# Squares and sums of the attention output on ScalarE, epsilon on GpSimd, and VectorE's small steps of two heads interleaved

## The chip, the cores and the metric

The kernel runs on one core of one Trainium2 chip. The metric is the device time in microseconds of one execution, the median over the runs. TensorE, VectorE, ScalarE and GpSimd each work through their own list of instructions in order and wait for one another by semaphores; the profile calls them PE (with PEld for its weight loads), DVE, ACT and POOL.

## The reference, cut to what matters

The program is a backbone of two layers over 256 context tokens and 1024 latent tokens, width 1024. Each layer mixes its tokens by four parallel groups and then runs a SwiGLU network. The change touches one of the groups, differential attention with four heads, 32 wide in queries and keys and 64 wide in values:

```
s = einsum('bhcqd,bhckd->bhcqk', q, k) * 32 ** -0.5      # c = 0, 1: two score maps per head
p = softmax(s, axis=-1)
w = p[:, :, 0] - lam * p[:, :, 1]
o = einsum('bhqk,bhkd->bhqd', w, v)
# then, per token and head, over the 64 values:
y = o * rsqrt(mean(o * o) + 1e-5) * g_subln * (1 - lam_init)
```

Latent queries read all 1280 keys. Context queries read the 256 context keys, and only in layer 0. All else of the layer (projections, retention, pooling, convolution, the network) is untouched.

## The kernel before, in words

Attention runs in three stretches ("runs"): in layer 0 the context tokens (2 tiles of 128 queries, 256 keys) and then the latent tokens (8 tiles, 1280 keys), in layer 1 the latent tokens alone (8 tiles). Within a run each engine has a hardware loop over the tiles; the first tile, and on TensorE the last, is written out ahead of or behind it. One lap handles the four heads of one tile, and each engine has its own fixed order of work, with older heads mixed in. `back(r, h, n)` names the head n before head h of tile r.

For one head the work passes through the engines like this:

- TensorE computes both score maps into PSUM (`scores`, L998).
- VectorE takes the maximum of each map (`maxima`, L2128), and for the first map it makes the exponential's bias from it (L2135). For the second map ScalarE makes the bias itself (L1559).
- ScalarE takes the exponentials and, by its accumulator, their sums (`exps`, L1565).
- VectorE (`combine`, one head later) takes the reciprocals of both sums (L2142), the ratio `beta` (L2143), and one pass over the keys that makes the weights of both maps together (L2147), released by semaphore `w`. The factor 1/sum of the first map is left for later, in `rinv` (L2150, once a tile).
- TensorE transposes the weights, 128 keys at a time (`turn`, L1016), ScalarE copies them out of PSUM (L1576), TensorE multiplies them with the values (`values`, L1028), and ScalarE copies the head's output (L1583).

When the four heads of a tile are done, its output is finished within the next lap, between that lap's heads 2 and 3:

- TensorE brings it to token-major form (`token_major`, L1036), in head 2.
- VectorE multiplies by `rinv` (`out_sum`, L2154), squares (L2157), sums over 64 (L2158), scales and adds epsilon (L2159), all behind the second maximum of head 2.
- GpSimd raises to the power -1/2 (L2699).
- VectorE multiplies by it (`out_norm`, L2166), behind the first maximum of head 3.
- TensorE transposes the result (`turn_out`, L1055), ScalarE writes its high 16-bit part with the gain (`out_hi`, L1587), VectorE the low part (`out_lo`, L2171).

TensorE's order within head 3 is: transposes for head 1, second score map of head 3, `turn_out`, first transposes for head 2, first score map of the next tile, then the modulation's matmuls (L926, a projection for a later part of the layer, fed in small pieces; in layer 0 heads 0, 1 and 3 have a piece, in layer 1 all four) and the values of head 1. The modulation of head 3 waits for `out_lo`, because both use one PSUM bank. A second small piece of the modulation (L933) stands ahead of the scores, and ScalarE copies its rows (L1501).

Semaphores for waits within an engine go through a small class, `Chain`: `link` raises the engine's own semaphore at the end of an instruction and waits for it at once; `enter` and `leave` keep its count over a hardware loop, whose raises per lap are stated as `per`.

## Time and profile before

| | us |
|---|---|
| Median of 3 runs | 3162.82 |
| Lowest and highest | 3156.35, 3166.67 |
| The profiled execution | 3156.76 |
| Its span in the profile | 3154.9 |
| TensorE busy | 2883.1 |
| VectorE busy | 1951.7 |
| ScalarE busy | 1238.2 |
| GpSimd busy | 561.6 |
| Mean granted TensorE clock, share of full speed | 0.961 |

The span is that of the instructions in the trace; the time of the execution lies 1.9 us above it. In the trace every time is counted from the span's start. Attention lies at 480 to 731 us (layer 0) and 2136 to 2352 us (layer 1). A line of the timeline gives the start, the duration, the engine, the line of the kernel, the operation, what it writes and reads, how many instructions were merged, and in brackets how long the engine had been idle before it and what ended that.

### The profile page before, as it was taken

To read this page: it belongs to the slowest core of one execution; us is meant where nothing else is said; L and a number is where in the kernel's file an instruction comes from. 1 tells how busy PE (TensorE), PEld (TensorE's weight loads), DVE (VectorE), ACT (ScalarE), POOL (GpSimd) and SP (SyncE) were. 2 spreads that over 40 slices of the span, in tenths; PEclk is the share of its full clock that TensorE was granted. 3 is DMA by queue.
4 is the path that set the end of the run, shared out by engine and by line. 5 is a ranking of instruction groups with operands and counts; after the bars stand their busy time and mean duration, and the time that the engine had idled before them with its cause. 6 is when DMAs were issued, how large, how long until landed. Compare 5 with 4: busy or idle time off the path is not lost.

```text
span 3154.9 us, 47187 instructions
## 1 busy us (share of the span) xinstructions
PE 2883.1 (91%) x17730; PEld 1617.4 (51%) x17730; DVE 1951.7 (62%) x2706; ACT 1238.2 (39%) x2368; POOL 561.6 (18%) x449
## 2 busy tenths in 40 slices
PE   5999887888899999999998899987889999999997
PEld 3555643554545556757755554544554434444443
DVE  5976786882575304626646686778864673374765
ACT  5212456773543213313324311447753542231332
POOL 0021010001318101202212004010003160121211
PEclk8999996999999999999999799999989999999998
DMA  5211111221143321111141311113322432111133
GB/s 211 74 41 36 36 46 70 86 78 67 55 147 133 107 87 41 41 41 50 45 147 41 143 44 41 44 42 112 109 79 80 137 103 76 51 56 52 54 140 115
DMA packets 69316, 248.95 MB, mean 79 GB/s; under 512 B 9248, under 2 KB 10016, under 8 KB 69152
## 3 DMA queue, kind: packets, MB, share of 16 engines
q1 hardware_dynamic: 68000, 241.44, 22.6%
q10 hardware_dynamic: 1152, 5.24, 0.4%
q8 instruction: 112, 1.84, 0.2%
q14 instruction: 52, 0.43, 0.0%
HBM read 221.75 MB, written 19.92 MB: 77 GB/s over the span
## 4 chain that ended last, share of the span: by engine, by line
PE 60%; issue 20%; DVE 11%; ACT 5%; DMA 2%; POOL 1%; SPq 0%; DVEq 0%; POOLq 0%; ACTq 0%
PE PS L801 38%; PE PS L970 16%; DVE wlo L1925 3%; PE PS L822 2%; DVE R L2102 1%; ACT whi L1418 1%; DVE R L2089 1%; PE PS L1175 1%; ACT SW L1776 1%; DMA R<-in_w_ada 1%; DMA stage<-in_w_gu 1%; ACT X L1535 1%; ACT R L1533 1%; DVE X L2378 1%; PE PS L1220 1%
## 5 line engine op out<-in xcount | busy, mean ns | idle before, releaser
L801 PE MATMUL PS<-R,whi 128*128 128x512 f16 (+1 forms) x4992 | 1359.2, 360 | 47.1 <-DVE wlo L1925 30.8
L801 PE MATMUL PS<-R,wlo 128*128 128x512 f16 (+1 forms) x2496 | 896.4, 359 | 0.0
L801 PEld LDWEIGHTS PS<-R,whi 128*128 128x128 f16 x4992 | 487.5, 99 | 550.8 <-issue 51.7
L970 PE MATMUL PS<-R,whi 128*128 128x256 f16 (+2 forms) x2352 | 510.2, 326 | 0.3 <-DVE wlo L1938 0.3
L1925 DVE SCALAR_TENSOR_TENSOR wlo<-stage,whi 128x1024 f16<-128x1024 f32 (+1 forms) x204 | 283.4, 1390 | 362.0 <-ACT whi L1418 361.1
L801 PEld LDWEIGHTS PS<-R,wlo 128*128 128x128 f16 x2496 | 246.2, 99 | 242.5 <-issue 10.7
L970 PE MATMUL PS<-R,wlo 128*128 128x256 f16 (+2 forms) x1176 | 319.1, 326 | 0.0
L970 PEld LDWEIGHTS PS<-R,whi 128*128 128x128 f16 x2352 | 230.1, 98 | 152.5 <-DVE wlo L1938 0.8
L1418 ACT ACTIVATE whi<-stage 128x1024 f16<-128x1024 f32 (+1 forms) x204 | 210.4, 1032 | 135.3 <-PE PS L801 85.0
L2128 DVE TENSOR_REDUCE tiny<-PS 128x1 f32<-128x1280 f32 (+1 forms) x144 | 197.1, 1369 | 37.4 <-PE PS L998 35.7
L1954 DVE TENSOR_TENSOR X<-X,PS 128x256 f32<-128x256 f32 (+2 forms) x294 | 150.8, 549 | 93.4 <-PE PS L970 93.2
L2616 POOL TENSOR_TENSOR X<-X 128x512 f32<-128x512 f32 (+1 forms) x89 | 121.6, 1370 | 384.4 <-ACT X L1818 290.9
L1565 ACT ACTIVATE R<-PS,tiny 128x1280 f32<-128x1280 f32 (+1 forms) x144 | 177.8, 1235 | 9.9 <-DVE tiny L2135 7.6
L2743 POOL TENSOR_TENSOR X<-stage 128x512 f32<-128x512 f32 x28 | 36.0, 1287 | 799.0 <-DMA stage<-in_w_gu 799.0
L2284 DVE SCALAR_TENSOR_TENSOR R<-X,small,R 128x1024 f32<-128x1024 f32 (+1 forms) x180 | 173.4, 1012 | 1.8
L970 PEld LDWEIGHTS PS<-R,wlo 128*128 128x128 f16 x1176 | 115.1, 98 | 76.0
L1436 ACT ACTIVATE whi<-X 128x512 f16<-128x512 f32 x112 | 70.0, 627 | 193.1 <-PE PS L970 90.9
L998 PE MATMUL PS<-R 128*128 128x512 f16 (+1 forms) x400 | 111.3, 362 | 34.6 <-ACT R L1576 22.9
L1016 PE MATMUL PS<-ident,R 128*128 128x128 f32 x656 | 106.1, 293 | 35.3 <-DVE R L2147 33.6
L1938 DVE SCALAR_TENSOR_TENSOR wlo<-X,whi 128x512 f16<-128x512 f32 x112 | 91.4, 818 | 51.6 <-ACT whi L1436 51.6
L1576 ACT ACTIVATE R<-PS 128x512 f32<-128x512 f32 (+1 forms) x200 | 97.2, 519 | 52.1 <-PE PS L1016 44.7
L2147 DVE SCALAR_TENSOR_TENSOR R<-R,tiny 128x1280 f32<-128x1280 f32 (+1 forms) x72 | 103.2, 1433 | 8.3
(227 smaller groups left out, 3570.3 us busy)
## 6 DMA issues: line engine op xcount, KB each, us to landing
stage<-in_w_gu SPq DMA_DIRECT2D x120, 512.0 KB, 3.8
X<-in_w_ada SPq DMA_DIRECT2D x60, 512.0 KB, 3.3
stage<-in_w_down SPq DMA_DIRECT2D x48, 512.0 KB, 3.4
stage<-in_w_in SPq DMA_DIRECT2D x44, 512.0 KB, 3.3
stage<-in_w_out SPq DMA_DIRECT2D x32, 512.0 KB, 3.2
h_save<-R SPq DMA_DIRECT2D x24, 640.0 KB, 5.3
R<-h_save SPq DMA_DIRECT2D x24, 640.0 KB, 4.9
T<-in_w_ada SPq DMA_DIRECT2D x20, 512.0 KB, 3.6
```

What stands on the lines that cost most here:

```text
L801: last = mm(slot(into, t0, t1)[:, c0 - t0:c1 - t0], w[:, j, k, :], row, start=(k == 0 and q == 0), stop=(k == K - 1 and q == 2))
L970: last = mm(s_bank(nf, t, o, n), w[:, j, k0 + k, :], row, start=(k == 0 and x == 0), stop=(k == PAIRS - 1 and x == 2))
L998: last = mm(slot(c)[:, k0:k1], Qst[:, 2 * h + c, bass.ds((t_first + r) * P, P)], Kst[:, 2 * h + c, k0:k1], start=True, stop=True)
L1016: last = nc.tensor.transpose(o[:, i * P:(i + 1) * P], Wt[h % 2][:, (k0 + i) * P:(k0 + i + 1) * P], ident[:, :])
L1418: A(whi[:, j, 0:K, :], stage[:, j, 0:K, :], ACT.Copy, scale=WS).then_inc(S["w_hi"], 1)
L1565: A((P1, P2)[c][h % 2][:, 0:keys], slot(c)[:, 0:keys], ACT.Exp, scale=SCORE, bias=nbias[:, h % 2, c:c + 1], accum_out=den[:, h % 2, c:c + ...
L1925: STT(wlo[:, j, 0:K, :], stage[:, j, 0:K, :], WS, whi[:, j, 0:K, :], ALU.mult, ALU.subtract).then_inc(S["w_lo"], 1)
L1954: last = TT(s_temp(l, dst)[:, o:o + w], s_temp(l, src)[:, o:o + w], s_bank(nf, t, o, w), ALU.add)
L2128: red = RED(smax[:, h % 2, c:c + 1], slot(c)[:, 0:keys], AX.X, ALU.max)
L2147: STT(Wt[h % 2][:, 0:keys], P2[h % 2][:, 0:keys], beta[:, 0:1], P1[h % 2][:, 0:keys], ALU.mult, ALU.add).then_inc(s("w"), 1)
L2284: STT(acc, src, wv, acc, ALU.mult, ALU.add).then_inc(S["conv"], 1)
L2616: TT(xrow(0)[:, a0:a1], xrow(0)[:, a0:a1], xrow(2 + d % 2)[:, a0:a1], ALU.add).then_inc(S[used], 1)
```

## The change

ScalarE gets the squares and sums of the tile's output (`out_squares`): four instructions, one for each head, Square with a scale of 1/8, so that the accumulated sum is already the mean over 64. They stand at the start of head 3 in ScalarE's order, ahead of the copies of older heads. GpSimd adds epsilon before its power. VectorE's `out_sum` keeps only its multiplication.

VectorE's order changes too. The reciprocal of the head before now stands between the first maximum and its bias, the ratio behind the bias, and `rinv` between the ratio and the pass that makes the weights. The waits within the engine are split into a raise (`mark`) and a later wait (`reach`), so that another instruction can stand between. `out_norm` moves from ahead of the weights' pass to behind it.

```diff
+    def mark(self, ins):
+        ins.then_inc(self.s, 1)
+        self.k += 1
+        return self.k
+
+    def reach(self, k):
+        self.eng.wait_ge(self.s, self.base + k)
...
 ScalarE
+                def out_squares(r):
+                    act.wait_ge(S["o_sum"], r + (done + 1))
+                    for h in range(HA):
+                        last = A(AO[:, 1, h, :], AO[:, 0, h, :], ACT.Square, scale=0.125, accum_out=st8[:, 0, h:h + 1])
+                    last.then_inc(S["o_sq"], 1)
+
                 def tile(r, first=False):
                     for h in range(HA):
+                        if h == 3 and not first:
+                            out_squares(r - 1)
                         if h == 3 or not first:
                             headed(*back(r, h, 3))
...
                 pv_copy(nt - 1, 3)
+                out_squares(nt - 1)
                 out_hi(nt - 1)
...
 VectorE
-                    own.link(red)
+                    return own.mark(red)
+
+                def bias(r, h, maximum):
+                    n = 4 * r + h
+                    own.reach(maximum)
                     if not (isinstance(r, int) and n < 2):
                         dve.wait_ge(s("exps"), 2 * n - 3 + before("exps"))
                     TS(nbias[:, h % 2, 0:1], smax[:, h % 2, 0:1], -SCORE, lamv[:, 12 + l:13 + l],
                        ALU.mult, ALU.add).then_inc(s("nbias"), 1)
 
-                def combine(r, h):
+                def inverse(r, h):
+
+                    dve.wait_ge(s("exps"), 2 * (4 * r + h) + 2 + before("exps"))
+                    return own.mark(nc.vector.reciprocal(rec[:, h, :], den[:, h % 2, :]))
+
+                def combine(r, h, inverted):
 
                     n = 4 * r + h
-                    dve.wait_ge(s("exps"), 2 * n + 2 + before("exps"))
-                    own.link(nc.vector.reciprocal(rec[:, h, :], den[:, h % 2, :]))
-                    own.link(STT(beta[:, 0:1], den[:, h % 2, 0:1], lamv[:, 10 + l:11 + l], rec[:, h, 1:2], ALU.mult, ALU.mult))
+                    own.reach(inverted)
+                    ratio = own.mark(STT(beta[:, 0:1], den[:, h % 2, 0:1], lamv[:, 10 + l:11 + l], rec[:, h, 1:2], ALU.mult, ALU.mult))
+                    if h == HA - 1:
+                        own.mark(TS(rinv, rec[:, :, 0], 1.0 / XS, None, ALU.mult))
+                    own.reach(ratio)
...
                     STT(Wt[h % 2][:, 0:keys], P2[h % 2][:, 0:keys], beta[:, 0:1], P1[h % 2][:, 0:keys],
                         ALU.mult, ALU.add).then_inc(s("w"), 1)
-                    if h == HA - 1:
-                        own.link(TS(rinv, rec[:, :, 0], 1.0 / XS, None, ALU.mult))
...
-                    dve.wait_ge(S["o_sum"], r + (done + 1))
-                    own.link(TT(AO[:, 1, :, :], AO[:, 0, :, :], AO[:, 0, :, :], ALU.mult))
-                    own.link(RED(st8[:, 0, 0:4], AO[:, 1, :, :], AX.X, ALU.add))
-                    TS(st8[:, 1, 0:4], st8[:, 0, 0:4], 1.0 / DV, 1e-5, ALU.mult, ALU.add).then_inc(S["o_var"], 1)
...
                     for h in range(HA):
-                        maxima(r, h, 0)
+                        maximum = maxima(r, h, 0)
+                        if h or not first:
+                            inverted = inverse(*back(r, h, 1))
+                        bias(r, h, maximum)
+                        if h or not first:
+                            combine(*back(r, h, 1), inverted)
                         if h == 3 and not first:
                             out_norm(r - 1)
-                        if h or not first:
-                            combine(*back(r, h, 1))
                         maxima(r, h, 1)
...
 GpSimd
                     with pool.Fori(0, nt) as r:
-                        pool.wait_ge(S["o_var"], r + (done + 1))
+                        own.enter(r, 1)
+                        pool.wait_ge(S["o_sq"], r + (done + 1))
+                        own.link(TT(st8[:, 1, 0:4], st8[:, 0, 0:4], epsv[:, 1:2].to_broadcast([P, 4]), ALU.add))
                         TT(st8[:, 2, 0:4], st8[:, 1, 0:4], nhalf[:, 0:1].to_broadcast([P, 4]),
                            ALU.pow).then_inc(S["o_pow"], 1)
+                    own.leave(nt, 1)
```

## Rows read from the trace of the kernel before

**Rows 1.** The page, busy time by engine over the whole span.
```profile
PE 2883.1 (91%) x17730; PEld 1617.4 (51%) x17730; DVE 1951.7 (62%) x2706; ACT 1238.2 (39%) x2368; POOL 561.6 (18%) x449
```
**Rows 2.** Windows between two GpSimd powers: stretch, length, busy by engine, clock, DMA.
```profile
632.55:657.22 24.67, 19.73 (x212) 13.29 (x210) 21.96 (x32) 19.26 (x41) 1.00 (x1) 1.00 0.25 90
657.22:683.45 26.23, 21.22 (x212) 14.56 (x210) 21.97 (x32) 19.27 (x41) 1.01 (x1) 0.93 0.24 85
2203.08:2227.84 24.76, 20.31 (x231) 13.82 (x228) 22.00 (x32) 19.42 (x42) 1.01 (x1) 1.00 0.33 112
```
**Rows 3.** Timeline of one lap of layer 1, around head 3.
```profile
2201.44 0.70 PE L998 MATMUL PS<-R 128*128 128x512 f16 x3
2201.47 0.41 DVE L2154 TENSOR_TENSOR R<-PS,st 128x256 f32<-128x256 f32 x1
...
2203.08 1.49 DVE L2128 TENSOR_REDUCE tiny<-PS 128x1 f32<-128x1280 f32 x1
2203.08 1.01 POOL L2699 TENSOR_TENSOR st<-st,tiny 128x4 f32<-128x4 f32 x1 [25.20 <-DVE st L2159]
2203.34 0.20 ACT L1565 ACTIVATION_READ_ACCUMULATOR R<-PS,tiny 128x1 f32 x1
...
2204.08 0.28 ACT L1501 ACTIVATE SW<-PS 128x128 f32<-128x128 f32 x1 [0.55 <-PE PS L1028]
...
2205.16 0.16 DVE L2142 RECIPROCAL st<-tiny 128x2 f32<-128x2 f32 x1
...
2205.42 1.33 ACT L1565 ACTIVATE R<-PS,tiny 128x1280 f32<-128x1280 f32 x1
...
2205.71 0.39 PE L1055 MATMUL PS<-ident,R 128*128 128x128 f32 x2
2205.71 1.55 DVE L2147 SCALAR_TENSOR_TENSOR R<-R,tiny 128x1280 f32<-128x1280 f32 x1
...
2207.40 0.65 PE L1016 MATMUL PS<-ident,R 128*128 128x128 f32 x4 [1.30 <-DVE R L2147]
...
2208.03 0.70 PE L998 MATMUL PS<-R 128*128 128x512 f16 x3
...
2208.58 0.47 DVE L2171 SCALAR_TENSOR_TENSOR R<-PS,small,R 128x256 f32 x1
...
2209.16 0.65 PE L926 MATMUL PS<-X,cpad 128*32 128x128 f32 x16 [0.43 <-issue]
```
**Rows 4.** The same timeline, from head 0 to head 1 of the following tile.
```profile
2213.72 0.21 ACT L1565 ACTIVATION_READ_ACCUMULATOR R<-PS,tiny 128x1 f32 x1
...
2214.42 0.70 PE L998 MATMUL PS<-R 128*128 128x512 f16 x3
...
2215.16 1.49 DVE L2128 TENSOR_REDUCE tiny<-PS 128x1 f32<-128x1280 f32 x1 [0.62 <-PE PS L998]
...
2218.41 1.33 ACT L1565 ACTIVATE R<-PS,tiny 128x1280 f32<-128x1280 f32 x1
```
**Rows 5.** Timeline of ScalarE in the retention stage of layer 0.
```profile
411.11 0.24 ACT L1776 ACTIVATE SW<-T 128x64 f32<-128x64 f32 x1
...
411.35 0.24 ACT L1776 ACTIVATE SW<-T 128x64 f32<-128x64 f32 x1
```
**Rows 6.** View of the exponential's line: duration min/median/max, first and last start.
```profile
L1565 ACT ACT_TABLE_LOAD  x2: 1283/1283/1283, 479.2 to 2136.2; - x2
```
**Rows 7.** Groups of GpSimd instructions by shape: count, busy us, mean ns, idle before.
```profile
L2616 POOL TENSOR_TENSOR X<-X 128x512 f32<-128x512 f32 x69 | 86.2, 1251 | 304.4 <-ACT X L1818 242.7 <-ACT X L1522 60.0
...
L2720 POOL TENSOR_TENSOR R<-R 128x256 f32<-128x256 f32 x4 | 2.7, 672 | 0.3
```
**Rows 8.** Timeline at the end of layer 1's attention run.
```profile
2349.86 0.42 DVE L2166 TENSOR_TENSOR R<-R,st 128x256 f32<-128x256 f32 x1 [1.12 <-POOL st L2699]
```
**Rows 9.** Timeline of the context run's one lap, layer 0.
```profile
499.93 0.19 ACT L1565 ACTIVATION_READ_ACCUMULATOR R<-PS,tiny 128x1 f32 x1
...
501.30 0.43 DVE L2166 TENSOR_TENSOR R<-R,st 128x256 f32<-128x256 f32 x1 [0.56 <-POOL st L2699]
```

More of the change, by code:

```diff
@@ L269, in build @@
               "slot_free act_own dve_own pool_own h_in out_done y_sq_ready y_sq_used h_sq_ready h_sq_used sumsq mean_sq root diag spread inv u_scaled u_hi u_done h_rows h_saved h_back "
-              "o_ps o_sum o_var o_pow o_norm ot_ps ot_hi ot_done").split()}
+              "o_ps o_sum o_sq o_pow o_norm ot_ps ot_hi ot_done").split()}
         S |= {n: sem(n) for n in PER_LAYER}
@@ L2155, in out_sum, with out_norm @@
                        rinv[:, :].rearrange("p (h e) -> p h e", e=1).to_broadcast([P, HA, DV]), ALU.mult).then_inc(S["o_sum"], 1)
+                def out_norm(r):
                     dve.wait_ge(S["o_sum"], r + (done + 1))
-                    own.link(TT(AO[:, 1, :, :], AO[:, 0, :, :], AO[:, 0, :, :], ALU.mult))
-                    own.link(RED(st8[:, 0, 0:4], AO[:, 1, :, :], AX.X, ALU.add))
-                    TS(st8[:, 1, 0:4], st8[:, 0, 0:4], 1.0 / DV, 1e-5, ALU.mult, ALU.add).then_inc(S["o_var"], 1)
-                def out_norm(r):
                     dve.wait_ge(S["o_pow"], r + (done + 1))
@@ L2186, in tile @@
                             out_lo(r - 1)
-                per = 4 + 8 + 1 + 2
+                per = 4 + 8 + 1
                 tile(0, first=True)
@@ L2194, in attend @@
                 own.leave(nt - 1, per)
-                combine(nt - 1, HA - 1)
+                combine(nt - 1, HA - 1, inverse(nt - 1, HA - 1))
                 out_sum(nt - 1)
```

## The prediction

> **What bounds the kernel now.** Read the page first: TensorE is busy for 91% of the span, VectorE for 62% and ScalarE for 39% [rows 1]. The change touches only the attention stage, so the question is what bounds that stage; the view of windows cut from one GpSimd root to the next gives it. A lap (one tile of 128 queries, four heads) of 1280 keys takes 24.67 us in layer 0 and 24.76 us in layer 1, VectorE busy for 22.0 of it, ScalarE for 19.3 and TensorE for 20 [rows 2]. Nobody is full: the lap is a ring of waits, to be read from the timeline of one lap.
>
> In the plain heads the ring runs through TensorE and ScalarE. The exponential's accumulator is read until 2213.92, the next scores start at 2214.42, and then come values, transposes and their copies until the next exponential of the same kind at 2218.41 [rows 4]. The span from one end to that start is 4.49 us; with 1.41 us of exponential and read it makes 5.90 us a head. VectorE waits 0.62 us for TensorE in it, so making VectorE faster there buys nothing.
>
> Head 3 is the other kind: 24.76 - 3 x 5.90 = 7.06 us, 1.16 us more. There VectorE holds the output sum (2201.47), the squares, sums and epsilon, and only then the maximum at 2203.08, though the scores ended at 2202.14. Its weights come at 2205.71 + 1.55 = 2207.26, and TensorE, idle for 1.30 us, starts the transposes at 2207.40. Then the scores of the next tile start at 2208.03, the low output part ends on VectorE at 2209.05, and the modulation's matmuls, which wait for it, start at 2209.16 [rows 3]. VectorE's chain sets this head twice.
>
> **What the change does, in layer 1's lap.** Three VectorE instructions leave each tile, which filled the 1.20 us from 2201.88 to the maximum at 2203.08. (a) The maximum of head 3 no longer waits for them. It starts when the scores are there: 2201.44 + 0.70 = 2202.14, plus the 0.04 us that the same pair shows in head 1 (2215.12 to 2215.16) [rows 3, 4], so 2202.18, and ends at 2203.67, where it ended at 2204.56.
>
> (b) From the maximum's end to the weights it was 1.15 us. The normalising multiply moves behind the weights (0.34 us net, by the 0.41 of an instruction of its shape less an overlap of 0.08), and the reciprocal (0.19 from its start to its follower's) slips into the wait for the maximum [rows 3]. That leaves 0.62 us: weights from 2204.29 to 2205.85. If the interleaving hides nothing it is 2206.05; I take the first. The reciprocal now stands ahead of the bias and waits for an exponential of the head before, read until 2203.54, 0.13 us before it is needed; the bias is needed at 2205.42 only, so this wait costs nothing up to some 1.5 us. The Trainium skill (VectorE: DVE Perf Modes, The DRAIN you can't avoid) says that instructions on VectorE gain nothing by being issued without semaphores between them; by that the weights would end at 2206.05 and the modulation start some 0.1 us later.
>
> (c) ScalarE gains four squares with sums. The trace has this operation on the same 128x64 shape: pairs of square and read start every 0.24 us (411.11, 411.35) [rows 5], so four take 0.97 us. They stand behind the exponential read until 2203.54, where ScalarE used to be idle for 0.55 us. The last sum is there at 2204.50, and the copies that started at 2204.08 start at 2204.40 [rows 3]: 0.32 us late. Everything behind them on ScalarE moves by that, so exponential (3,0) starts at 2205.74 and is read until 2207.15. Between 0 (all idle) and 0.97 (no idle) I take 0.32; layer 0's laps without a modulation at head 2 have less idle, so up to 0.7 there, but they also have the longer wait of TensorE to win back, and I price them alike.
>
> (d) GpSimd gains the addition of epsilon, 128x4, which no row shows. Additions there take 672 ns for 256 columns and 1251 for 512 [rows 7]: 2.26 ns a column, so about 0.1 us for 4. From above, the only 128x4 row is the power, 1.01 us [rows 3]. I take 0.1 plus 0.07 for the link, because two rows of the same operation point there, and keep 1.01. Then the power runs from about 2204.75 to 2205.76. The Trainium skill (GPSIMD Engine Reference, Performance versus the Vector engine) puts two software dispatch hops on each instruction here and makes elementwise work VectorE's; that speaks for the dearer end, and with it the root would come at 2206.7.
>
> (e) The normalising multiply starts when weights and root are there, 2205.8, and ends at 2206.22. TensorE turns the output 0.14 us later (the delay that 2207.26 to 2207.40 shows), for 0.39 us, and the transposes of head 2 follow until about 2207.25. Scores of the next tile: 0.50 us behind the exponential's read [rows 4], 2207.65, where it was 2208.03. The second maximum of head 3 runs 2206.22 to 2207.7, the low output part 2207.65 to 2208.1, and no longer holds the modulation, which follows the scores' 0.70 us with a small overlap, at about 2208.29. It was 2209.16 [rows 3]: **0.87 us a lap**. The check by the ring: head 3 is now 5.90 + 0.32 = 6.2 us, where it was 7.06. What is late next is the TensorE and ScalarE ring itself, which is why the saved 1.2 us of VectorE work and the 0.2 us in each other head are not worth more.
>
> Where each layer runs eight tiles, seven laps hold this work of the tile before: 14 x 0.87 = 12.2 us. What stands outside it:
> - Three run ends, where the chain lies bare (VectorE waits 1.12 us for the root [rows 8]). Before, 1.20 us passed from the output sum's end (2201.88) to the power's start (2203.08); now 0.05 to ScalarE, 1.06 of squares, 0.08 to GpSimd, 0.17 of addition: 1.36. That is +0.16 each, +0.5 in all; with the dear addition +3.2.
> - The one lap of the context run (256 keys). VectorE waited 0.56 us for the root even before, at 501.30. The exponential ahead of the squares is read until 500.12, so the root comes at 500.12 + 0.97 + 0.08 + 0.17 + 1.01 = 502.35 and the multiply 1.1 us later than before [rows 9]: +1.1.
>
> Net without the clock: -12.2 + 0.5 + 1.1 = -10.6 us.
>
> **The clock.** A lap at mean granted clock 1.00 takes 24.67 us, the next one at 0.93 takes 26.23 [rows 2]. Six of the 12 full laps between one tile's root and the next have 0.93, and cost 0.8 to 1.6 us each, 7.8 together; each time the fall to the lower level (1.2 GHz) follows head 3, where TensorE idled longest. That idle time, 1.30 + 0.43 us in layer 1, shrinks by about 0.9. So between none and all six go; I take three, -4.5 us, since the fall came only in some laps with the same idle time. Forecast: **-15 us**, 0.5%. Against the profiled execution (3156.76 us, span 3154.9) that is 3142; against the median of 3162.82, which is 6 us above the profiled one, 3148.
>
> **Rivals.**
> 1. The root comes late. If the addition costs 1.01 us the multiply starts at 2206.7, and because it stands in VectorE's order ahead of the second maximum and on TensorE ahead of the transposes, everything of (e) moves with it: maximum to 2208.6, low part to 2209.05, modulation at 2209.16, just as before. Gain per lap 0, run ends and context +5, clock unchanged: about 3168. For it: the 1.01 us row. Against: the two rows of additions. 13%.
> 2. ScalarE's squares are paid in full (0.97 instead of 0.32): the lap gains 0.2 us, 3 us in all; with run ends and the context lap 3161. For it: ScalarE lies in the ring of every head. Against: the 0.55 us of idle before 2204.08. 9%.
> 3. The lap gains, but the lower clock level comes in more laps than six: without any change of the clock the time is 3152, with two laps more 3155, with all 12 (+6 x 1.4) 3161. For it: other stretches of the head get denser waits. Against: the fall follows the longest idle, which shrinks. 12%.
> 4. The other side: the square needs another activation table than the exponential. One load is 1.28 us [rows 6], two a lap 2.57 us on ScalarE inside the ring. From 0.9 us of added ScalarE time per lap the sign turns; here 2.57 - 0.87 = 1.7 us more in 14 laps, and 6 us at the context lap and run ends: 3193. Against: the exponential's line has two loads in the whole execution, one for each layer, though squares run on ScalarE later under the same table. 4%. The Trainium skill (ScalarE: Activation LUTs, Table sets) names square in no set but says that cheap functions are in every one; the two loads agree with that.
>
> **Chances.** Forecast 62%, rivals 13, 9, 12 and 4%. 0.3% (9.5 us) is what a measurement of this kernel can tell from no change, so faster means below 3153.3. Faster: nearly all of the forecast, a third of rivals 2 and 3: 0.68. Same 0.26, slower 0.06. Range: the low end is the forecast with all six clock falls gone (-10.6 - 7.8 = -18.4, 3144) less 5 us for medians that differ by such; the high end, 3161, takes in rivals 2 and 3, and leaves out 1 and 4.
>
> **What would show it.** In the timeline of a lap of layer 1: maximum of head 3 within 0.8 us of the output sum's start; four squares every 0.24 us, ending about 1 us behind the read; an addition of about 0.1 us on GpSimd (at 1 us rival 1 holds); the copies at head 3 about 0.3 us later against the read than now; TensorE's idle before the transposes of head 2 gone; laps of about 23.9 us at clock 1.00, plain heads still 5.90. In the table by lap, fewer than six at 0.93. Loads still two on the exponential's line. It is wrong if plain heads change length, or if the multiply behind the weights is found waiting for GpSimd.

## The result: 0.4% slower

The changed kernel takes 3174.49 us (median of 6 runs, 3168.87 to 3176.29). The kernel before, run beside it, takes 3162.86 us (6 runs, 3155.49 to 3166.67). The ratio is 1.004, with an interval of 1.0026 to 1.0053: slower by 11.6 us. The prediction said 3148 with a range up to 3161, and gave slower a chance of 0.06. It was wrong, in sign too.

The profiled execution of the changed kernel took 3176.29 us (span 3174.5), 19.5 more than the profiled one of before. The page's busy times first:

```profile
PE 2896.6 (91%) x17730; PEld 1626.4 (51%) x17730; DVE 1928.7 (61%) x2652; ACT 1251.8 (39%) x2512; POOL 579.5 (18%) x467
```

VectorE is busy for 23 us less and ScalarE for 14 us more than in [rows 1], as planned. The work was moved. The time went elsewhere. Cut by stage, from the exponential's table load to the end of the last low output part, layer 0's attention grew from 251.5 to 261.5 us and layer 1's from 215.9 to 222.3; all the rest grew by 3.1. So the laps have to be read. The windows from one GpSimd power to the next, as in [rows 2]:

```profile
641.37:668.73 27.36, 22.12 (x208) 15.12 (x208) 21.01 (x28) 19.97 (x49) 2.32 (x3) 0.88 0.22 81
2219.87:2246.33 26.46, 21.73 (x226) 14.68 (x226) 21.01 (x28) 20.07 (x50) 2.32 (x3) 0.94 0.29 104
2273.20:2298.50 25.30, 20.24 (x226) 13.84 (x226) 20.98 (x28) 20.07 (x50) 2.32 (x2) 1.00 0.30 109
```

The one lap at clock 1.00 takes 25.30 us, where it was 24.76 and should have been 23.89. VectorE is busy for 1.0 us less in it and still the lap is longer. And 11 of the 12 laps now hold a fall of the clock, where it was 6; some stand at 0.88. The timeline of head 3 of a layer 1 lap shows why, against [rows 3].

```profile
2215.36 0.41 DVE L2180 TENSOR_TENSOR R<-PS,st 128x256 f32<-128x256 f32 x1
2216.09 1.49 DVE L2145 TENSOR_REDUCE tiny<-PS 128x1 f32<-128x1280 f32 x1 [0.32 <-PE PS L1006]
2217.35 0.25 ACT L1601 ACTIVATE R<-R 128x64 f32<-128x64 f32 x1
...
2218.18 1.55 DVE L2175 SCALAR_TENSOR_TENSOR R<-R,tiny 128x1280 f32<-128x1280 f32 x1
2218.30 0.26 ACT L1509 ACTIVATE SW<-PS 128x128 f32<-128x128 f32 x1
2218.48 1.31 POOL L2726 TENSOR_TENSOR st<-st,tiny 128x4 f32<-128x4 f32 x1 [24.08 <-ACT R L1601]
2219.87 1.01 POOL L2727 TENSOR_TENSOR st<-st,tiny 128x4 f32<-128x4 f32 x1
2221.07 0.43 DVE L2189 TENSOR_TENSOR R<-R,st 128x256 f32<-128x256 f32 x1 [1.33 <-POOL st L2727]
...
2221.64 0.41 PE L1063 MATMUL PS<-ident,R 128*128 128x128 f32 x2 [1.81 <-DVE R L2189]
```

The maximum (L2145) starts 0.73 us behind the start of the output sum (L2180), where it was 1.61. The squares (L1601) follow, and the weights' pass (L2175) starts 2.82 us behind the output sum's start, where it was 4.24. Up to here all is as predicted. Then GpSimd's addition of epsilon (L2726) starts 0.30 us into the pass and takes 1.31 us, for four columns. It ends 0.06 us behind the pass, here and in all 14 laps of this trace where it starts inside one. The power follows, and VectorE has stood still for 1.33 us when the multiply can start, with the second maximum queued behind it. TensorE stands for 1.81 us before it turns the output (L1063), with head 2's transposes queued behind that. Four-column additions of the same line take 0.20 us where no such pass runs, as at the end of the run and in the context lap:

```profile
2367.44 0.42 DVE L2180 TENSOR_TENSOR R<-PS,st 128x256 f32<-128x256 f32 x1 [9.32 <-PE PS L1044]
2369.04 0.20 POOL L2726 TENSOR_TENSOR st<-st,tiny 128x4 f32<-128x4 f32 x1 [16.82 <-ACT R L1601]
2369.31 1.01 POOL L2727 TENSOR_TENSOR st<-st,tiny 128x4 f32<-128x4 f32 x1
2370.41 0.42 DVE L2189 TENSOR_TENSOR R<-R,st 128x256 f32<-128x256 f32 x1 [2.55 <-POOL st L2727]
```
```profile
501.14 0.42 DVE L2180 TENSOR_TENSOR R<-PS,st 128x256 f32<-128x256 f32 x1 [0.92 <-PE PS L1044]
...
503.67 0.20 POOL L2726 TENSOR_TENSOR st<-st,tiny 128x4 f32<-128x4 f32 x1 [38.87 <-ACT R L1601]
...
505.08 0.43 DVE L2189 TENSOR_TENSOR R<-R,st 128x256 f32<-128x256 f32 x1 [1.46 <-POOL st L2727]
```

### The profile page after: what moved, and what is told of

Its sections match the earlier page's. It is cut to its first block, busy times and chain, and to the rows that moved or that the text cites. A ratio compares the mean times of both kernels' runs of the same rounds, so it can differ in the third digit from the quotient of the medians.

```text
span 3174.5 us, 47289 instructions
## 1 busy us (share of the span) xinstructions
PE 2896.6 (91%) x17730; PEld 1626.4 (51%) x17730; DVE 1928.7 (61%) x2652; ACT 1251.8 (39%) x2512; POOL 579.5 (18%) x467
## 4 chain that ended last, share of the span: by engine, by line
PE 59%; issue 20%; DVE 11%; ACT 5%; DMA 2%; POOL 2%; SPq 1%; POOLq 0%; DVEq 0%; ACTq 0%
PE PS L809 38%; PE PS L978 14%; DVE wlo L1942 2%; PE PS L830 2%; DVE R L2119 1%; ACT whi L1426 1%; PE PS L1183 1%; DVE R L2106 1%; DMA stage<-in_w_gu 1%; ACT SW L1793 1%; DMA R<-in_w_ada 1%; POOL st L2726 1%; ACT R L1541 1%; ACT X L1543 1%; DVE X L2404 1%
## 5 line engine op out<-in xcount | busy, mean ns | idle before, releaser
L2145 DVE TENSOR_REDUCE tiny<-PS 128x1 f32<-128x1280 f32 (+1 forms) x144 | 197.4, 1371 | 56.0 <-PE PS L1006 53.1
L1584 ACT ACTIVATE R<-PS 128x512 f32<-128x512 f32 (+1 forms) x200 | 97.3, 520 | 29.4 <-PE PS L1024 24.7
L2175 DVE SCALAR_TENSOR_TENSOR R<-R,tiny 128x1280 f32<-128x1280 f32 (+1 forms) x72 | 103.2, 1433 | 6.7
```

The costliest lines, as they stand in the source:

```text
L2145: red = RED(smax[:, h % 2, c:c + 1], slot(c)[:, 0:keys], AX.X, ALU.max)
L2175: STT(Wt[h % 2][:, 0:keys], P2[h % 2][:, 0:keys], beta[:, 0:1], P1[h % 2][:, 0:keys], ALU.mult, ALU.add).then_inc(s("w"), 1)
```

## The experiments

Each experiment set theory **P** against others. P: the pass over the weights holds every GpSimd instruction that falls into it, and the late root that follows is the loss. The others, by the letters of the expectations:

- **A** (1 to 4): the addition costs 1.3 us by itself.
- **S** (called B in 4 to 6): ScalarE's squares, in the ring of every head, are what lengthens the lap.
- **C** in 6 to 8: the interleaving, or the multiply's place behind the pass, costs the time.
- **D** (9): VectorE's queue, blocked by its wait for the root, is the loss.
- **K** (called C in 12): the falls of the clock alone make the difference.

The kernel before was measured again beside each group of experiments, with medians of 3163.34 us (1 to 4), 3165.20 (5 to 8), 3161.84 (9 to 11) and 3162.50 (12). The ratios are to these, so compare ratios across groups and not medians.

**1. The addition alone, beside the pass and not.** The kernel before, with two additions of 128x4 on GpSimd per tile that nobody waits for:

```diff
+   root_of_tile(r)
+   own.link(TT(st8[:, 1, 4:8], epsv.., nhalf.., ALU.add))   # behind the power
+   pool.wait_ge(S["scores"], 8 * r + (16 + ...))            # released inside the pass
+   own.link(TT(st8[:, 0, 4:8], epsv.., nhalf.., ALU.add))
```

> The kernel before with two small GpSimd additions more in each tile but the last, both 128x4 with the same operands: one right behind the power (VectorE then reduces from PSUM), one released by the second score map of head 3, which falls into VectorE's pass that makes the weights (two inputs from SBUF, 1.55 us). Theory P (GpSimd is held while that pass runs): the first takes about 0.2 us, the second 0.8 to 1.4 us and ends with the pass. Rival A (an addition in such a loop costs 1.3 us by itself): both 1.3 us. Time of the kernel the same within 3 us in either case, since nobody waits for them.

Measured: 3163.10 us (one run; before 3163.34). The timeline of a layer 1 lap:

```profile
2209.83 0.20 POOL L2705 TENSOR_TENSOR st<-tiny 128x4 f32<-128x4 f32 x1
...
2211.48 1.55 DVE L2147 SCALAR_TENSOR_TENSOR R<-R,tiny 128x1280 f32<-128x1280 f32 x1
2211.73 1.36 POOL L2707 TENSOR_TENSOR st<-tiny 128x4 f32<-128x4 f32 x1 [1.70 <-PE PS L998]
```

The same instruction takes 0.20 us during the maximum, which reads PSUM, and 1.36 us when it starts inside the pass (L2147), and it ends with the pass (2213.09 against 2213.03). Of the 15 in the trace, six start inside the pass, 0.17 to 0.29 us behind its start; they take 1.32 to 1.44 us, and each ends 0.06 us behind it. The other nine start ahead of it, or within 0.02 us of its start, and take 0.20 to 0.27. So it isn't slowed, it is held, and A is out. P has its mechanism, and since nobody waits for it here, it costs nothing.

**2. No addition.** The changed kernel with the power reading the sums directly (epsilon is left out):

```diff
-   own.link(TT(st8[:, 1, 0:4], st8[:, 0, 0:4], epsv.., ALU.add))
-   TT(st8[:, 2, 0:4], st8[:, 1, 0:4], nhalf.., ALU.pow)
+   TT(st8[:, 2, 0:4], st8[:, 0, 0:4], nhalf.., ALU.pow)
```

> The changed kernel without GpSimd's addition of epsilon (epsilon left out of the output's norm); the power reads the sums at once. Theory P: the power is now what is held by the weights' pass, it is shown with up to 2.3 us, its result comes as late as now to within 0.3 us, and the kernel gains at most 0.3 us in each of 14 laps: 3170 to 3175. Rival A: the power runs 1.0 us from the squares' end, the root comes 1.4 us earlier, VectorE does not wait for it: 3145 to 3155, faster than before.

Measured: 3160.88 us (10 runs), 0.9999 of before (0.9988 to 1.0011).

```profile
2208.38 1.55 DVE L2175 SCALAR_TENSOR_TENSOR R<-R,tiny 128x1280 f32<-128x1280 f32 x1
...
2208.68 2.12 POOL L2725 TENSOR_TENSOR st<-st,tiny 128x4 f32<-128x4 f32 x1 [24.21 <-ACT R L1601]
...
2210.99 0.42 DVE L2189 TENSOR_TENSOR R<-R,st 128x256 f32<-128x256 f32 x1 [1.05 <-POOL st L2725]
```

Now the power is the one that is held: 2.12 us where it took 1.01 in [rows 3]. The multiply starts 2.39 us behind the squares' end, against 2.67 in the change and 1.30 forecast. So the hold doesn't belong to the addition. The time misses what P expected (3170 to 3175) by 9 us, and what A expected (3145 to 3155) by 6: TensorE waits 1.54 us where it waited 1.81, the lap at full clock is 25.04 instead of 25.30, and 8 laps fall instead of 11. A quarter of a microsecond of the wait was worth more than its own length.

**3. The addition behind the pass.** The changed kernel with one more wait, so that the addition starts when the pass has ended:

```diff
    pool.wait_ge(S["o_sq"], r + (done + 1))
+   pool.wait_ge(S["w"], 4 * r + (7 + ...))
```

> The changed kernel, with GpSimd's addition released only when the weights' pass is over (a wait for its semaphore, in all tiles but the last). Theory P: the addition takes 0.2 us, the root is 0.1 to 0.3 us later than in the changed kernel, time +0 to +5 us against it. Rival A: the addition still takes 1.3 us, now all behind the pass: +1.3 us in each of 14 laps, 3190 or more.

Measured: 3178.39 us (5 runs), 1.0051 (1.0031 to 1.0071).

```profile
2219.59 1.55 DVE L2175 SCALAR_TENSOR_TENSOR R<-R,tiny 128x1280 f32<-128x1280 f32 x1
...
2221.22 0.20 POOL L2727 TENSOR_TENSOR st<-st,tiny 128x4 f32<-128x4 f32 x1 [25.64 <-DVE R L2175]
...
2222.70 0.43 DVE L2189 TENSOR_TENSOR R<-R,st 128x256 f32<-128x256 f32 x1 [1.56 <-POOL st L2728]
```

The addition takes 0.20 us again. The root is no sooner there, since the 1.31 us was waiting and not work. A had expected 3190 or more. The median is 3.9 us above the changed kernel's, and the lap at full clock is 25.53 us for 25.30, by the added link; the two intervals overlap, so that the whole kernel is slower than the changed one is not shown.

**4. Squares and epsilon moved, VectorE's order left as before** (the multiply ahead of the weights):

```diff
 def out_sum(r):
-   own.link(TT(AO[:, 1], AO[:, 0], AO[:, 0], ALU.mult))
-   own.link(RED(st8[:, 0, 0:4], AO[:, 1], AX.X, ALU.add))
-   TS(st8[:, 1, 0:4], st8[:, 0, 0:4], 1.0 / DV, 1e-5, ...)
 # ScalarE: out_squares(r - 1) at head 3, GpSimd: the addition, as in the change
```

> The kernel before with one part of the change: squares on ScalarE and epsilon on GpSimd, VectorE's order as before (normalising multiply ahead of the reciprocals and the weights' pass, no interleaving). Theory P: VectorE waits for the root and runs no pass meanwhile, so the addition takes 0.2 us and the root is there at about 2.3 us behind the last exponential's read; the weights' pass of head 3 comes 1.2 to 1.5 us later than before, laps of 25.8 to 26.3 us at full clock: 3178 to 3190, slower than the changed kernel. Rival A: the addition takes 1.3 us here too, 3195 or more. Rival B (ScalarE's squares in its ring are the loss, not the late root): laps like the changed kernel's, 25.3 us.

Measured: 3183.73 us (4 runs), 1.0078 (1.0055 to 1.0101), as P expected. All additions take 0.20 us, since the pass now starts behind the root; VectorE waits 2.03 us for that root, and all 12 laps hold a fall of the clock. Squares behind the exponential make the root late in either order. Here VectorE waits ahead of the weights, in the change behind them.

**5. The changed kernel, squares one head earlier** (`out_squares(r - 1)` at the end of head 2, ahead of its second exponential, and not at head 3).

> The changed kernel with one move: ScalarE's four squares ahead of the second exponential of head 2 instead of behind it, so that GpSimd's two instructions are over before VectorE's weights' pass begins. The same work on every engine. Theory P (the late root, held by the pass, is the loss): addition 0.2 us, root there before the pass ends, VectorE does not wait for it, TensorE's transposes of head 2 about 5.3 us behind that exponential's place instead of 5.9; laps of layer 1 at full clock 24.3 to 24.7 us (changed: 25.30, before: 24.76), fewer laps with a clock fall: 3153 to 3163. Rival B (ScalarE's added work in its ring is the loss): laps stay at 25.3 us or longer, since the exponential now starts 1 us later: 3172 or more.

Measured: 3158.99 us (12 runs), 0.9981 (0.9969 to 0.9992).

```profile
2229.38 0.41 DVE L2180 TENSOR_TENSOR R<-PS,st 128x256 f32<-128x256 f32 x1
...
2230.97 0.20 POOL L2726 TENSOR_TENSOR st<-st,tiny 128x4 f32<-128x4 f32 x1 [25.16 <-ACT R L1601]
...
2231.25 1.01 POOL L2727 TENSOR_TENSOR st<-st,tiny 128x4 f32<-128x4 f32 x1
...
2232.47 0.17 DVE L2162 RECIPROCAL st<-tiny 128x2 f32<-128x2 f32 x1 [0.86 <-ACT R L1573]
...
2233.13 1.55 DVE L2175 SCALAR_TENSOR_TENSOR R<-R,tiny 128x1280 f32<-128x1280 f32 x1
...
2234.60 0.42 DVE L2189 TENSOR_TENSOR R<-R,st 128x256 f32<-128x256 f32 x1
```

The addition takes 0.20 us and the root is there at 2232.26, long before the pass ends. The ratio falls from the change's 1.0040 to 0.9981, with the same work on every engine. S had expected 3172 or more. But the lap at full clock is 24.77 to 24.80 us, no shorter than before, and just above what P expected; attention as a whole is 3.8 us longer in this trace than in that of before, so the small gain over before is not shown to lie there. The squares now stand in front of an exponential whose sums the reciprocal needs: VectorE waits 0.86 us for it, and the pass starts 3.75 us behind the output sum instead of 2.82.

**6. The same squares with VectorE's old order** (experiment 4 with the squares at head 2).

> The kernel before with squares on ScalarE ahead of the second exponential of head 2 and epsilon on GpSimd; VectorE's order as before, the normalising multiply ahead of the reciprocals. Theory P: root there when the bias of head 3 is made, so the multiply waits little; TensorE's turn of the output is done early and the transposes of head 2 start about 0.5 us earlier than in the kernel before: laps of 24.2 to 24.5 us, 3148 to 3160, the best of these. Rival B: 3170 or more. Rival C (interleaving and moving the multiply behind the pass is what costs): this one clearly faster than e5, by 5 us or more.

Measured: 3147.80 us (6 runs), 0.9947 (0.9931 to 0.9963), the fastest of the kernels that leave nothing out, and 0.2 us below the range expected.

```profile
2199.19 0.20 POOL L2705 TENSOR_TENSOR st<-st,tiny 128x4 f32<-128x4 f32 x1 [23.27 <-ACT R L1593]
...
2199.47 1.01 POOL L2706 TENSOR_TENSOR st<-st,tiny 128x4 f32<-128x4 f32 x1
...
2200.67 0.43 DVE L2171 TENSOR_TENSOR R<-R,st 128x256 f32<-128x256 f32 x1 [0.53 <-POOL st L2706]
...
2203.25 0.65 PE L1016 MATMUL PS<-ident,R 128*128 128x128 f32 x4 [0.93 <-DVE R L2156]
```

The squares' end to the multiply is 1.56 us, VectorE waits 0.53 us, TensorE 0.93 us ahead of the transposes (1.30 before), laps are 24.55 and one of 12 holds a fall.

It is 11.2 us faster than experiment 5, more than the 5 us that C asked for. So with the early squares VectorE's order in head 3 does cost: in 5 the interleaved reciprocal stands ahead of the bias and waits 0.86 us for the exponential behind the squares, and in 6 it stands behind the multiply and waits for nothing. In the changed kernel this wait does not exist, since the squares stand behind that exponential.

**7 and 8. The interleaving alone**, squares, sums and epsilon on VectorE as before; in 7 the multiply stands ahead of the weights, in 8 behind them.

```diff
 # 8: the change without out_squares, with the three VectorE instructions back in out_sum
 # 7: and out_norm(r - 1) ahead of combine(...)
```

> The kernel before with the interleaving of reciprocal, bias and ratio alone; squares, sums and epsilon stay on VectorE, the multiply ahead of the pass. Theory P: this part is harmless; the weights' pass of head 3 starts 0.2 us earlier, laps of 24.5 to 24.7 us at full clock, 3156 to 3163. Rival C: slower than before, 3168 or more. By the view that instructions on VectorE gain nothing without waits between them: the pass starts no earlier, 3163.

> As e7, but with the normalising multiply behind the weights' pass as in the changed kernel; squares and sums still on VectorE, GpSimd's power alone, which runs while VectorE reduces from PSUM. Theory P: power 1.0 us, root early, no wait on VectorE; weights 0.5 us earlier, TensorE's turn of the output 1.5 us later than before but just in time, laps of 24.5 to 24.8 us: 3158 to 3166. Rival C (the place of the multiply is the loss): laps of 25.2 us or more, 3170 or more.

Measured: 3151.82 us (5 runs; 0.9957, 0.9941 to 0.9972) and 3151.62 us (4 runs; 0.9953, 0.9935 to 0.9972). Both beat what I expected by 4 us and more. Laps at full clock are 24.53 and 24.66 against 24.76, and 2 and 5 laps hold a fall. The interleaving alone is worth 13 us (3165.20 beside it), with the multiply in either place. C is out as a cause of the change's loss, which is all in the part that moved the squares and epsilon.

**9. The multiply behind the second maximum** in the changed kernel:

```diff
     combine(*back(r, h, 1), inverted)
-    if h == 3 and not first:
-        out_norm(r - 1)
     maxima(r, h, 1)
+    if h == 3 and not first:
+        out_norm(r - 1)
```

> The changed kernel with the normalising multiply moved behind the second maximum of head 3, so that VectorE does not stand still for the root. Theory P: GpSimd's addition is still held until the pass ends, the root is as late as before, and TensorE, whose turn of the output stands ahead of the transposes of head 2, waits just as long; at most 0.2 us a lap is won: 3168 to 3175. Rival D (the loss is that VectorE's queue is blocked by the wait): the second maximum is 1.4 us earlier and laps go to 24.3 us or less: 3150 to 3160.

Measured: 3175.91 us (5 runs), 1.0049 (1.0032 to 1.0065).

```profile
2215.82 1.55 DVE L2175 SCALAR_TENSOR_TENSOR R<-R,tiny 128x1280 f32<-128x1280 f32 x1
2216.11 1.31 POOL L2726 TENSOR_TENSOR st<-st,tiny 128x4 f32<-128x4 f32 x1 [24.18 <-ACT R L1601]
...
2217.50 1.01 POOL L2727 TENSOR_TENSOR st<-st,tiny 128x4 f32<-128x4 f32 x1
2218.90 0.41 DVE L2189 TENSOR_TENSOR R<-R,st 128x256 f32<-128x256 f32 x1
...
2219.46 0.41 PE L1063 MATMUL PS<-ident,R 128*128 128x128 f32 x2 [2.01 <-DVE R L2189]
```

VectorE waits for no root any more. TensorE does: 2.01 us before L1063, because that stands ahead of head 2's transposes in its order. The lap at full clock is 25.47 us, so nothing was won, not even the 0.2 us that P allowed. D, which expected 3150 to 3160, is out.

**10. Early squares, interleaving in heads 0 to 2.** Experiment 6 with the reciprocal, bias and ratio interleaved in the other heads.

> A version that the runs point to: as e6 (squares ahead of the second exponential of head 2, multiply ahead of the reciprocal in head 3), plus the changed kernel's interleaving in the other heads. Theory P: head 3 as in e6, the other heads have no use for the 0.2 us; within 3 us of e6, 3144 to 3152, faster than before. If interleaving helps by itself in all heads: 3140 or less.

Measured: 3148.24 us (6 runs), 0.9958 (0.9945 to 0.9972). As experiment 6: laps 24.53, one holds a fall. In the other heads the interleaving shows no gain.

**11. Is it the two inputs?** Experiment 1 with a pass of one input, a tensor_scalar of the second map (the first map's weights are left out).

> The first probe with the weights' pass reading one SBUF tensor instead of two (the first map's weights are left out of the computation). Theory P in its narrow form (only a pass with two SBUF inputs holds GpSimd): the addition inside it takes 0.2 us, as the one behind the power. In its wide form (any pass of VectorE from SBUF holds it): it ends with the pass. The pass itself may be shorter, 0.7 to 1.5 us.

Measured: 3138.88 us (one run).

```profile
2216.25 0.89 DVE L2147 TENSOR_SCALAR R<-R,tiny 128x1280 f32<-128x1280 f32 x1
```
```profile
2216.52 0.67 POOL L2707 TENSOR_TENSOR st<-tiny 128x4 f32<-128x4 f32 x1 [1.72 <-PE PS L998]
```

The pass is over in 0.89 us, 0.70 ns a column where the other takes 1.21, and still the addition inside it ends with it (2217.19 against 2217.14), at 0.67 us instead of 0.20. So a pass with one input holds GpSimd too, at least in this quicker form. The kernel's time shows something else as well: with the pass 0.66 us shorter TensorE idles 0.60 us in head 3 where it was 1.30, the lap is 24.08 us where it was 24.76, and no lap holds a fall.

**12. The changed kernel without its root's wait.** All is as in the change, but in the long runs the multiply reads an earlier tile's root, so the right scale of the output is left out:

```diff
+   old_root = sb("old_root", [P, 4])
-   if h == 3 and not first: out_norm(r - 1)
+   if h == 3 and not first: out_norm(r - 1, old_root[:, :] if nt > 2 else None)
    ...
+   own.link(TS(old_root[:, :], st8[:, 2, 0:4], 1.0, None, ALU.mult))   # behind out_lo
```

> The changed kernel with VectorE's normalising multiply reading the root of an earlier tile, out of a buffer of its own, in both long attention runs, so that it waits for no root of its own tile (this leaves out the right scale of the attention output; GpSimd still adds and powers, and VectorE copies its root, 128x4, at the end of head 3, long after it is there). Everything else, ScalarE's squares at head 3 and the interleaving, is as in the change. It asks whether the prediction's steps (a), (b), (c) and (e) were right once the root is taken out: then the multiply starts at the end of the weights' pass, 4.35 us behind the start of the output sum, a lap of layer 1 at full clock is near the 23.89 us of the prediction plus up to 0.1 for the copy, TensorE's idle time at the turn of the output is under 0.6 us, most laps keep the full clock, and the time is near 3148. If instead ScalarE's squares and the exponential behind them set head 3 (rival S), the lap stays at 24.5 to 24.8 us as in the kernels with early squares, though VectorE waits for nothing, and the time is 3155 to 3165. If the lap shortens but laps still fall to the lower clock (rival C), single laps are at 23.9 and the others near 25.5, and the time is 3150 to 3160.

Measured: 3135.56 us (4 runs), 0.9921 (0.9904 to 0.9937).

```profile
2209.29 0.41 DVE L2181 TENSOR_TENSOR R<-PS,st 128x256 f32<-128x256 f32 x1
...
2212.11 1.55 DVE L2176 SCALAR_TENSOR_TENSOR R<-R,tiny 128x1280 f32<-128x1280 f32 x1
...
2212.41 1.31 POOL L2731 TENSOR_TENSOR st<-st,tiny 128x4 f32<-128x4 f32 x1 [21.44 <-ACT R L1602]
...
2213.58 0.42 DVE L2192 TENSOR_TENSOR R<-R,old_root 128x256 f32<-128x256 f32 x1
...
2214.14 0.41 PE L1064 MATMUL PS<-ident,R 128*128 128x128 f32 x2 [0.39 <-DVE R L2192]
```
```profile
2237.64:2261.53 23.89, 20.50 (x226) 13.87 (x226) 20.92 (x30) 20.11 (x50) 2.38 (x3) 1.00 0.33 115
```

The addition is held as in the change, but nobody waits for it. The multiply starts 4.29 us behind the output sum, TensorE idles 0.39 us, a full lap of layer 1 is 23.84 to 23.97 us, and none of 12 holds a fall. S is out: ScalarE's squares are all still at head 3. The time is 12 us below what the prediction's mechanism gave. In the trace all falls have gone and not three, and the last stretch of each run is shorter too (from the root before last to the last one 18.97 and 21.33 us before, at granted clocks of 0.91 and 0.76; 13.97 and 13.84 here, at 1.00 and 0.99). My expectation had missed both.

## Why the prediction was wrong

The failed step is **(d), GpSimd's addition**, priced at 0.1 + 0.07 us, with 1.01 as its upper end. Bare it takes 0.20. In the lap it takes 1.31 and ends after the pass. With (d) the root's place in (e) falls: the multiply starts not at the end of the weights but 1.34 us behind it. The sum from the squares' end to the multiply was 1.30 us (2204.50 to 2205.8); it is 2.67 (2218.40 to 2221.07), 1.37 more. That is 1.22 for the addition (0.25 us from the squares' end to the power's start forecast, 1.47 measured) and 0.15 from the power's end to the multiply. At full clock the lap is 1.41 us longer than forecast, 25.30 against 23.89: the same figure within 0.04. It is also what the prediction named as its refutation: the multiply behind the weights, found waiting for GpSimd.

Experiment 12 takes this one wait out and gives the forecast's lap, 23.84 to 23.97 against 23.89. So the other steps held:

- **(a)** The maximum started 0.73 us behind the output sum; 0.71 was forecast.
- **Plain heads** kept their length, 5.87 to 5.93 us from one head's scores to the next, as before. The prediction's 7.06 us for head 3 is a lap less three plain heads and no interval of the trace: in [rows 3] and [rows 4] the scores around head 3 start 6.59 and 6.39 us apart (2201.44, 2208.03, 2214.42). The sum stands all the same; in experiment 12 one interval of 6.1 to 6.2 us is left and the others are plain.
- **(b)** The pass started 2.82 us behind the output sum, as forecast. The interleaving gains 0.2 us in a plain head: from the maximum's end to the pass 0.60 us, against 0.81 in [rows 4]'s lap (2215.16 + 1.49 to 2217.46).

```profile
2210.22 1.49 DVE L2145 TENSOR_REDUCE tiny<-PS 128x1 f32<-128x1280 f32 x1 [0.71 <-PE PS L1006]
...
2212.31 1.55 DVE L2175 SCALAR_TENSOR_TENSOR R<-R,tiny 128x1280 f32<-128x1280 f32 x1
```

- **(c)** Squares come every 0.24 us (2217.35, 2217.59), the copies at 2218.30, 1.04 us behind the exponential's read starts where it was 0.74 (2203.34 to 2204.08), so 0.30 late (forecast 0.32). Rival 2, the squares paid in full, is out.
- **Ends and context.** Output sum's end to the power's start is 1.45 us at the run's end (forecast 1.36), and 505.08 is 3.52 us behind the output sum's end, where [rows 9]'s lap had 2.26 (499.04 to 501.30): +1.26 (forecast +1.1).
- **Loads.** Two as in [rows 6], so rival 4 is out:

```profile
L1573 ACT ACT_TABLE_LOAD  x2: 1283/1283/1283, 481.9 to 2150.3; - x2
```

Rival 1 had the right chain, the multiply in order ahead of the second maximum and of the transposes, and took it only to 1.01 us, hence to a gain of nothing per lap. The bound itself was wrong. I took it from a free-standing row, the 128x4 power, which in [rows 3] starts with the maximum, though the addition would start inside the weights' pass. What such a neighbour does stood in the trace of before, in another stage, and I didn't look:

```profile
972.85 1.69 DVE L1925 SCALAR_TENSOR_TENSOR wlo<-stage,whi 128x1024 f16<-128x1024 f32 x1
973.53 1.53 POOL L2731 TENSOR_TENSOR R<-R 128x256 f32<-128x256 f32 x1
```

A GpSimd instruction of 128x256 takes 0.67 us in [rows 7]. This one, of the same shape, starts inside a VectorE pass of two SBUF inputs, takes 1.53, and ends 0.52 us behind it. Five more of that shape start inside such passes there and take 1.53 to 1.65. By this row the addition, forecast to start about 0.3 us into a pass of 1.55, comes to an estimated 1.2 us or more, and the multiply lands near where it was measured.

The Trainium skill speaks of it (SBUF — State Buffer, Who interferes with whom): a VectorE instruction with two SBUF inputs contends with a GpSimd instruction that reads SBUF, and the one that is issued first keeps the other out for its whole length. The trace agrees for the pass first (1.31 and 1.36 us), and shows no hold beside a VectorE instruction that reads PSUM (0.20 us beside the maximum). The other order is in the trace of before: this VectorE addition takes 1.23 us where the median of its line is 0.42, and it ends 0.28 us behind the GpSimd instruction that was there first.

```profile
434.95 1.09 POOL L2694 TENSOR_TENSOR R<-R,X 128x512 f32<-128x512 f32 x1 [83.82 <-DMA X<-in_ropeA]
435.09 1.23 DVE L2434 TENSOR_TENSOR R<-R 128x256 f32<-128x256 f32 x1
```

On experiment 11 the Trainium skill's same section says that a tensor_scalar contends when it runs in a mode that uses both ports, which goes with the pass's 0.70 ns a column.

**The clock** was the second term: -4.5 us was forecast, for fewer falls. Over the 12 laps of the change, 318.6 us in sum, 15.0 us are above 12 x 25.30; before it was 303.5 us, about 7 above 12 x 24.7. So it came as about +8. The place of the falls is as the prediction had it: in the laps of before and of the change each begins 5.2 to 8.2 us behind the output sum's start, in TensorE's idle time of head 3 or behind it. That idle time grew. By kernel, in order of the idle time (us) before the transposes of head 2 or the turn ahead of them, in a layer 1 lap; idle time, laps and falls are of the one profiled execution, medians and ratios of all:

| kernel | TensorE's idle | lap at clock 1.00 | laps of 12 below 1.00 | median | ratio to before |
|---|---|---|---|---|---|
| 12 old root | 0.39 | 23.89 | 0 | 3135.6 | 0.992 |
| 11 one-input probe | 0.60 | 24.08 | 0 | 3138.9 (one run) | |
| 10, 6 early squares, old order | 0.92, 0.93 | 24.53, 24.55 | 1, 1 | 3148.2, 3147.8 | 0.996, 0.995 |
| 7 interleaving, multiply ahead | 1.06 | 24.53 | 2 | 3151.8 | 0.996 |
| 8 interleaving, multiply behind | 1.28 | 24.66 | 5 | 3151.6 | 0.995 |
| 5 change, early squares | 1.29 | 24.77 | 6 | 3159.0 | 0.998 |
| 1 probe | 1.29 | 24.75 | 6 | 3163.1 (one run) | |
| before | 1.30 | 24.76 | 6 | 3162.9 | 1 |
| 2 no addition | 1.54 | 25.04 | 8 | 3160.9 | 1.000 |
| the change | 1.81 | 25.30 | 11 | 3174.5 | 1.004 |
| 9 multiply behind maximum | 2.01 | 25.47 | 10 | 3175.9 | 1.005 |
| 3 addition behind the pass | 2.04 | 25.53 | 11 | 3178.4 | 1.005 |

From the first row to the last the idle time grows by 1.65 us and the lap at full clock by 1.64. (Experiment 4, with two idle times of 0.70 and 1.60 us, has falls in all 12.) Rival 3 had the extra falls, with the lap itself gaining; the lap itself lost. K is half right: in the traces the clock doubles the loss of the laps (6.5 us without it, 15.1 with it), but the falls come in more laps with the wait that P makes, and are gone from the trace of experiment 12 with it.

Between the profiled executions the miss is 34.3 us (3176.29 against 3142): 14 x 1.41 = 19.7 for the lap at full clock, 12.4 for the clock (7.9 more where 4.5 less was forecast), and 2.2 in the rest. By the medians it is 26.5 us, since the profiled execution of before lay 6.1 us below its median and that of the change 1.8 above; how many laps fall in the other executions no trace shows. Nor does any show how the falls are decided inside a lap; two equal laps of one run can differ in it. That stays open. A version that keeps the change and hides the root, with TensorE's turn of the output one head later, was not tried; experiment 12 says what it could reach at best, 27 us.

## What to carry to other kernels

Before a small instruction goes to GpSimd, look at what VectorE runs at the moment of its start: inside a long SBUF pass its price is what is left of that pass, and part of its own time on top (0.06 us of the addition's 0.20, 0.87 of the power's 1.01). Price a moved step by rows taken beside the same kind of neighbour, from another stage if need be; where the trace has none, the bound is the neighbour's length, not the longest row of the same shape. And price a wait at TensorE above its length, where some laps of the loop already hold a clock fall and others don't.

## What the runs showed of the hardware

- GpSimd is held by a VectorE pass of two SBUF inputs until it ends: 1.27 to 1.44 us for an addition that takes 0.20 alone, 2.12 for a power that takes 1.01. Also by a one-input pass at 0.70 ns a column (0.67 us). Beside a maximum that reads PSUM the addition takes 0.20.
- The other way round, a VectorE addition of 128x256 with two SBUF inputs took 1.23 us instead of 0.42 when it started inside a GpSimd instruction of 1.09.
- An addition of 128x4 takes 0.20 us on GpSimd, the power of the same shape 1.01: at this size the operation makes a factor of five.
- In this loop more laps hold a fall of TensorE's granted clock below its full level (2.4 GHz) the longer TensorE idles in head 3: none of 12 at 0.39 us, one at 0.93, six at 1.30, eleven at 1.81, in one profiled execution each.
